# Two multiplications of constants at the head of each one-block expert

## The chip, the cores and the metric

The kernel runs on one core of a Trainium2 chip. Its time is device microseconds from the start to the end of one execution. TensorE (PE, with its weight loads PEld), VectorE (DVE), ScalarE (ACT), GpSimd (POOL) and SyncE (SP, which issues the transfers) have queues of their own and wait for each other by semaphores.

## The reference

Two transformer blocks over 256 tokens of 1024 values, all in float32. The first has two layers, the second of which ends in a mixture of experts; the second block is one further layer. The change is in the mixture:

```
def moe_swiglu(x, router_w, w1, w3, w2):
    t = x.reshape(B * S, D)
    logits = (t @ router_w).astype(jnp.float32)
    top_v, top_i = lax.top_k(logits, TOP_K)              # 2 of 8
    gates = jax.nn.softmax(top_v, axis=-1)
    combine = jnp.sum(one_hot(top_i, N_EXPERTS) * gates[..., None], axis=1)
    out = jnp.zeros_like(t)
    for e in range(N_EXPERTS):
        out = out + combine[:, e:e + 1] * swiglu(t, w1[e], w3[e], w2[e])
    return out

def swiglu(x, w1, w3, w2):
    return (jax.nn.silu(x @ w1) * (x @ w3)) @ w2
```

w1 and w3 of an expert are 1024 x 3584, w2 is 3584 x 1024.

## The kernel before

**Experts.** The eight experts are taken in order of the tokens they hold, the fullest first. For each the tokens that chose it are gathered into one or two blocks by a product with a matrix of picks (`gather`, `e_P`), go through the expert's three matrices, and are added back to the running sum `acc` (named b_XT in the trace) by another product (`finish`). `FORMS` gives the forms an expert may take. "n" is a plain block of up to 128 tokens. "a" is a folded block of up to 64 tokens, whose high and low parts lie side by side in one stationary operand. A form of two letters has two blocks. Which form of the list runs is chosen at run time from the counts.

**Pieces.** A weight matrix is multiplied as a high and a low part. SyncE loads 1 MB halves into four ring buffers; ScalarE rounds a piece of 128 x 2048 values to its high part (`e_hi`, line 2371), VectorE subtracts to get the low part (`e_lo`, line 1901), and TensorE multiplies both by the block: lines 993, 994 and 995 in a plain block (three products, 12 to a piece), lines 998 and 999 in a folded one (two products, 8 to a piece). There are places for three split pieces; ScalarE may split piece p when TensorE is done with p - 3 (`split_round`), VectorE follows (`split_rest`), TensorE waits for that (`take_piece`). ScalarE and VectorE are told to split p + 2 at the step in which TensorE takes p. An expert has 42 pieces. They come in units of 512 hidden columns (`steps_of`): w1 in two pieces into bank 0, w3 in two pieces into bank 2, then the hidden values are turned ("T", line 1017 or 629) and multiplied by two pieces of w2 into banks 4 and 5. In a folded block ScalarE copies bank 0 out, TensorE adds the two halves of the block up again (the doubling product, line 1077), and ScalarE takes SiLU of that.

**From one expert to the next.** During its last pieces an expert with one block gathers the next one's tokens into banks 0 and 2, and adds the expert before it back (`finish`, lines 1127 and 1128). After its last piece ScalarE scales the result out of banks 4 and 5 (`e_yh`), VectorE makes the rest (`e_yl`, line 1422), and, as there is no second block, VectorE's queue then raises the semaphores that a second block would have raised, `acc_add[1]` the last of them (line 2140). At its head each expert but the first waits on TensorE for `acc_add[1]` of the one before, then for its gathered rows (`gath_l[0]`), and then does its first product, into bank 0, which also waits for its piece.

**Multiplications of constants.** `keep_up(n, b)` multiplies the identity by the first 512 columns of the constants n times into bank b; nobody reads the result. The kernel has it at seven places outside the experts' loop (line 642). Each f32 multiplication leaves two records of a matmul in the trace.

The order of the instructions is written out by hand, each engine's in its own function.

Of the kernel before, what the change touches and what calls it, by code (L numbers as in the profile page):

```python
# [209 lines left out]
def block_of(ex, s):  # L210

    return (ex + s) % 2
# [57 lines left out]
def two_blocks(nc, a):  # L270
    ctx = ExitStack()
    with ctx:
# [344 lines left out]
        def pe(e):  # L617
# [21 lines left out]
            def keep_up(n, b):  # L639

                for _ in range(n):
                    e.matmul(bank[b][:, :], ident, cst[:, 0:512], start=True, stop=True)
# [461 lines left out]
            def gather(ex, s, g, b):  # L1104

                e.wait_ge(*pick[s](ex))
                for c in range(4):
                    ins = sums(bank[b][:, tok(c)], [(X[:, t, tok(4 * g + c)], e_P[s][:, t, :]) for t in range(2)])
                ins.then_inc(gath[s].sem)

            def turn_picks(ex, s, b):

                e.wait_ge(*pick[s](ex))
                turn(bank[b], [e_P[s][:, t, :] for t in range(2)])
                sums(bank[b][:, 256:257], [(e_P[s][:, t, :], comb[:, t, ex:ex + 1]) for t in range(2)]).then_inc(pt_turn[s].sem)

            def finish(ex, banks):

                e.wait_ge(*y_dve[0](ex))
                e.wait_ge(*y_act[0](ex))  # L1120
                if ex:
                    e.wait_ge(*acc_add[0](ex - 1))
                pt = e_PT[0][ex % 3]
                for t in range(2):
                    for n in range(2):
                        b = bank[banks[2 * t + n]]
                        e.matmul(b[:, :], pt[:, tok(t)], e_yh[:, half(n)], start=True, stop=False)
                        e.matmul(b[:, :], pt[:, tok(t)], e_yl[:, half(n)], start=False, stop=True).then_inc(back[0].sem)

            def finish_second(ex):  # L1130

                e.wait_ge(*y_dve[1](ex))
                e.wait_ge(*y_act[1](ex))
                for t in range(2):
                    for n in range(2):
                        e.matmul(bank[2 * t + n][:, :], e_PT[1][0][:, tok(t)], e_h[n][:, :], start=True, stop=True).then_inc(back[1].sem)

            def expert(ex, kinds, wide, hints, on):

                unit, more, tiles = 6 + 7 * ex, ex + 1 < NE, len(kinds)  # L1140
                if ex:
                    e.wait_ge(*acc_add[1](ex - 1))
                if tiles == 1:
                    e.sem_inc(gath[1].sem, 2)
                    e.sem_inc(pt_turn[1].sem, 1)
                    e.sem_inc(back[1].sem, 4)
                if tiles == 2 and ex:
                    e.wait_ge(*gath_l[0](ex))
                    e.wait_ge(*pt_out[0](ex))
                    if ex > 1:  # L1150
                        e.wait_ge(*acc_add[0](ex - 2))
                    for g in range(2):
                        gather(ex, 1, g, 2 + g)
                    turn_picks(ex, 1, 1)
                e.wait_ge(*gath_l[0](ex))

                def first(kind, s):
                    if kind == "w1":
                        return [gath_l[1](ex), pt_out[1](ex)] if s else []
                    if kind == "w3":  # L1160
                        return [gath_l[1](ex)] if s else [pt_out[0](ex)]
                    if ex and tiles == 2:
                        return [acc_add[0](ex - 1)]
                    return [y_dve[0](ex - 1), y_act[0](ex - 1)] if ex else []

                def aside(kind, u, hf):
                    if more and len(FORMS[ex + 1]) == 2 and kind == "T" and u == 3:
                        hints.append(e.mark_branch_hint_location(hint=wide[ex + 1]))
                    if tiles == 2 and kind == "T" and u == 6:
                        on.append(e.mark_branch_hint_location())  # L1170
                    if ex and tiles == 2 and (kind, u, hf) == ("w1", 0, 1):
                        finish(ex - 1, (4, 5, 6, 7))
                    if more and tiles == 1 and kind == "T" and u == 4:
                        if ex > 1:
                            e.wait_ge(*acc_add[0](ex - 2))
                        turn_picks(ex + 1, 0, 6)
                    if tiles == 1 and (kind, u, hf) == ("d", 5, 1):
                        if more:
                            gather(ex + 1, 0, 0, 0)
                            e.wait_ge(*tl_out(unit + 6))  # L1180
                            gather(ex + 1, 0, 1, 2)
                        if ex:
                            if more:
                                e.wait_ge(*pt_out[0](ex + 1))
                            finish(ex - 1, (6, 7, 1, 3))
                    if more and tiles == 2 and kind == "T" and u == 6:
                        for g in range(2):
                            gather(ex + 1, 0, g, g)
                        e.wait_ge(*tl_out(unit + 6))
                        turn_picks(ex + 1, 0, 2)  # L1190

                gated(FFE_UNITS, MOE_P + 42 * ex, unit, kinds, first, aside, [block_of(ex, s) for s in range(2)])
                if "a" not in kinds:
                    e.sem_inc(g_both.sem, 7)
                if tiles == 2:
                    if more:
                        e.wait_ge(*gath_l[0](ex + 1))
                        e.wait_ge(*pt_out[0](ex + 1))
                    finish_second(ex)

            def experts():
# [10 lines left out]
                for ex in range(NE):  # L1212
                    if len(FORMS[ex]) == 1:
                        expert(ex, FORMS[ex][0], wide, hints, [])
                        continue
                    branch = e.br_eq(wide[ex], 0, on_true=f"narrow{ex}", on_false=f"wide{ex}")
                    for place in hints:
                        branch.branch_hint(place)
                    hints = []
                    with nc.body(f"wide{ex}", valid_engines=[e.engine]):  # L1220
                        on = []
                        expert(ex, FORMS[ex][1], wide, hints, on)
                        end = e.br(f"done{ex}")
                        for place in on:
                            end.branch_hint(place)
                    with nc.body(f"narrow{ex}", valid_engines=[e.engine]):
                        on = []
                        expert(ex, FORMS[ex][0], wide, hints, on)
                        end = e.br(f"done{ex}")
                        for place in on:  # L1230
                            end.branch_hint(place)
                    nc.switch_bb(f"done{ex}")
# [1890 lines left out]
```

## Time and profile before

| | |
|---|---|
| median of 3 runs | 2141.49 us (2138.68 to 2147.89) |
| the profiled execution | 2139.3 us; span from first to last instruction 2137.5 us |
| busy in the span | PE 93%, PEld 73%, DVE 71%, ACT 52%, POOL 3% |
| mean granted clock of TensorE | 0.985 of full |
| chain that ended last, by engine | PE 72%, DVE 13%, issue 7%, ACT 7%, POOL 1% |
| records of line 642 (constants) | 94, that is 47 multiplications |
| experts 1 to 7, first product of 1 to last of 7 | 947.72 to 1783 us |

A busy PE is not PE at its peak. The chain is followed back from the last instruction, at each step to what released it. A share of the span is an average over stages with different limits, so the stretch around the change is read by itself.

### The profile page before, as it was taken

How to read it: one execution, taken by the hardware profiler on the slowest of the kernel's cores; microseconds unless marked ns; L12 is line 12 of the kernel's file. 1: busy time of each engine (PE TensorE's matmuls, PEld its weight loads, DVE VectorE, ACT ScalarE, POOL GpSimd, SP SyncE). 2: the span in 40 equal slices, each digit the busy share in tenths (PEclk: the TensorE clock that was granted, in tenths of full speed). 3: DMA queues.
4: the chain of work that ended last, by engine and by line, in shares of the span. 5: the costliest groups of instructions: out<-in, count | busy, mean ns of one | idle time of the engine just before them, and what ended most of it. 6: DMA issues, size and time to landing. Idle time of an engine off the chain costs nothing.

```text
span 2137.5 us, 25380 instructions
## 1 busy us (share of the span) xinstructions
PE 1998.2 (93%) x9950; PEld 1562.1 (73%) x9950; DVE 1511.9 (71%) x1835; ACT 1101.8 (52%) x1144; POOL 58.0 (3%) x64
## 2 busy tenths in 40 slices
PE   8989999999899999999999998988988898999997
PEld 7568588876596788878878766666666666659997
DVE  4665645447575655568888898998899898646666
ACT  1233244412230344447677777877777773545554
POOL 0120000000400000000000000000000000100000
PEclk9999999999999899999999999999999999999999
DMA  8201264433000666659989899999999994316450
GB/s 332 79 1 52 110 252 177 157 144 118 1 1 1 262 230 211 217 180 369 362 320 367 332 403 348 404 358 381 392 356 403 345 401 169 119 64 255 166 205 20
DMA packets 65018, 484.42 MB, mean 227 GB/s; under 512 B 9840, under 2 KB 12912, under 8 KB 13680
## 3 DMA queue, kind: packets, MB, share of 16 engines
q1 hardware_dynamic: 64880, 482.58, 59.6%
q8 instruction: 87, 1.43, 0.3%
q14 instruction: 51, 0.42, 0.1%
HBM read 481.51 MB, written 1.05 MB: 226 GB/s over the span
## 4 chain that ended last, share of the span: by engine, by line
PE 72%; DVE 13%; issue 7%; ACT 7%; POOL 1%; DMA 0%; DVEq 0%; SPq 0%; ACTq 0%; POOLq 0%
PE bank L622 12%; PE bank L993 11%; PE bank L995 11%; PE bank L994 11%; PE bank L998 7%; PE bank L999 6%; PE bank L825 5%; ACT e_hi L2371 4%; DVE e_lo L1901 4%; PE bank L1017 2%; PE bank L1077 2%; PE bank L786 1%; PE bank L629 1%; DVE b_arena L1416 1%; DVE e_h L1416 1%
## 5 line engine op out<-in xcount | busy, mean ns | idle before, releaser
L1901 DVE TENSOR_TENSOR e_lo<-b_ring,e_hi 128x2048 fp32r<-128x2048 f32 (+1 forms) x407 | 921.1, 2280 | 286.5 <-ACT e_hi L2371 285.5
L2371 ACT ACTIVATE e_hi<-b_ring 128x2048 fp32r<-128x2048 f32 (+1 forms) x407 | 772.1, 1909 | 200.2 <-PE bank L995 114.3
L998 PE MATMUL bank<-e_hi,e_x 128*128 128x512 f32 x672 | 277.9, 414 | 34.7 <-DVE e_lo L1901 24.8
L999 PE MATMUL bank<-e_lo,e_x 128*128 128x512 f32 x672 | 264.2, 393 | 0.0
L993 PE MATMUL bank<-e_hi,e_x 128*128 128x512 f32 (+1 forms) x528 | 209.6, 397 | 5.9 <-DVE e_lo L1901 4.4
L994 PE MATMUL bank<-e_lo,e_x 128*128 128x512 f32 (+1 forms) x528 | 203.8, 386 | 0.0
L995 PE MATMUL bank<-e_hi,e_x 128*128 128x512 f32 (+1 forms) x528 | 203.8, 386 | 0.0
L998 PEld LDWEIGHTS bank<-e_hi,e_x 128*128 128x128 f32 x672 | 126.7, 189 | 101.8 <-DVE e_lo L1901 60.9
L998 PE MATMUL bank<-e_hi,e_th 128*128 128x512 f32 x336 | 137.9, 410 | 20.7 <-DVE e_lo L1901 20.1
L999 PEld LDWEIGHTS bank<-e_lo,e_x 128*128 128x128 f32 x672 | 127.0, 189 | 25.0 <-issue 1.8
L993 PE MATMUL bank<-e_hi,e_th 128*128 128x512 f32 x352 | 137.8, 391 | 0.4 <-DVE e_tl L1905 0.4
L994 PE MATMUL bank<-e_lo,e_th 128*128 128x512 f32 x352 | 137.2, 390 | 0.0
L995 PE MATMUL bank<-e_hi,e_tl 128*128 128x512 f32 x352 | 137.1, 389 | 0.0
L999 PE MATMUL bank<-e_lo,e_th 128*128 128x512 f32 x336 | 131.6, 392 | 0.0
L622 PE MATMUL bank<-b_ring,b_XT 128*128 128x512 f32 (+1 forms) x320 | 128.3, 553 | 1.5 <-issue 1.5
L993 PEld LDWEIGHTS bank<-e_hi,e_x 128*128 128x128 f32 x528 | 100.4, 190 | 27.9 <-issue 9.2
L994 PEld LDWEIGHTS bank<-e_lo,e_x 128*128 128x128 f32 x528 | 100.4, 190 | 20.4 <-issue 1.7
L995 PEld LDWEIGHTS bank<-e_hi,e_x 128*128 128x128 f32 x528 | 100.1, 190 | 20.3
L2371 ACT ACTIVATE b_arena<-bank 128x512 f32<-128x512 f32 (+2 forms) x96 | 46.0, 511 | 132.3 <-PE bank L629 67.6
L993 PE MATMUL bank<-e_x,e_hi 128*128 128x256 f32 x384 | 108.9, 284 | 2.0 <-DVE e_x L1905 1.9
L995 PE MATMUL bank<-e_x,e_lo 128*128 128x256 f32 x384 | 108.7, 283 | 0.0
L994 PE MATMUL bank<-e_x,e_hi 128*128 128x256 f32 x384 | 108.7, 283 | 0.0
(268 smaller groups left out, 2852.8 us busy)
## 6 DMA issues: line engine op xcount, KB each, us to landing
b_ring<-in_moe_w SPq DMA_DIRECT2D x336, 1024.0 KB, 7.0
b_ring<-in_ffn_w SPq DMA_DIRECT2D x15, 2048.0 KB, 8.4
b_ring<-in_w_in SPq DMA_DIRECT2D x14, 2048.0 KB, 8.1
b_ring<-in_w_up SPq DMA_DIRECT2D x12, 2048.0 KB, 8.3
b_ring<-in_w_down SPq DMA_DIRECT2D x6, 2048.0 KB, 8.2
b_ring<-in_w_o SPq DMA_DIRECT2D x4, 2048.0 KB, 8.2
b_gain<-in_gains SPq DMA_DIRECT2D x6, 1024.0 KB, 4.5
b_ring<-in_w_out SPq DMA_DIRECT2D x2, 2048.0 KB, 8.5
```

The source lines that it names most:

```text
L622: ins = e.matmul(out, x, y, start=start and i == 0, stop=stop and i == len(pairs) - 1)
L825: last = e.matmul(heads(b)[:, h, :], *f(h), start=True, stop=True)
L993: e.matmul(out, ah, bh, start=first, stop=False)
L994: e.matmul(out, ah, bl, start=False, stop=False)
L995: return e.matmul(out, al, bh, start=False, stop=last)
L998: e.matmul(out, both, bh, start=first, stop=False)
L999: return e.matmul(out, both, bl, start=False, stop=last)
L1017: ins = e.matmul(bank[2 + s][:, 64 * c:64 * c + 64], e_h[s][:, tok(c)], pairs[:, 0:64], start=True, stop=True)
L1077: e.matmul(bank[s][:, 0:w], pairs, e_h[s][:, 0:w], start=True, stop=True).then_inc(g_both.sem)
L1416: return e.tensor_tensor(out, x, y, op)
L1901: e.tensor_tensor(lo, raw, r32(hi), ALU.subtract).then_inc(lo_dve.sem)
L2371: return e.activation(out, x, ACT.Copy)
```

## The change

Behind the two waits at the head of an expert that isn't the first and has one block, TensorE multiplies constants twice into bank 0. The first product after it starts a new sum in that bank.

```
                     turn_picks(ex, 1, 1)
                 e.wait_ge(*gath_l[0](ex))
+                if ex and tiles == 1:
+                    keep_up(2, 0)
 
                 def first(kind, s):
                     if kind == "w1":
```

TensorE's order at the head of a plain expert with one block (b_cst are the constants, e_x the gathered block; s_st_out carries `acc_add[1]`, s_dec_in `gath_l[0]`, s_lo_dve the low part; the branch closes the other form of the expert):

```order
-L1223 UNCONDITIONAL_BRANCH
-L993 MATMUL bank0<-e_hi0,e_x 128x512 [waits s_st_out,s_lo_dve,s_dec_in]
+L1225 UNCONDITIONAL_BRANCH
+L642 MATMUL bank0<-b_cst 128x512 [waits s_st_out,s_dec_in]
+L642 MATMUL bank0<-b_cst 128x512
+L993 MATMUL bank0<-e_hi0,e_x 128x512 [waits s_lo_dve]
 L994 MATMUL bank0<-e_lo0,e_x 128x512
```

The two waits have moved from the first product to the first multiplication of constants; the product keeps its wait for the piece. TensorE's order at the head of a folded expert, the eighth:

```order
-L1229 UNCONDITIONAL_BRANCH
-L998 MATMUL bank0<-e_hi0,e_x 128x512 [waits s_st_out,s_lo_dve,s_dec_in]
+L1231 UNCONDITIONAL_BRANCH
+L642 MATMUL bank0<-b_cst 128x512 [waits s_st_out,s_dec_in]
+L642 MATMUL bank0<-b_cst 128x512
+L998 MATMUL bank0<-e_hi0,e_x 128x512 [waits s_lo_dve]
 L999 MATMUL bank0<-e_lo0,e_x 128x512
```

The same two come in front here, before the pairs of lines 998 and 999. No other engine's order changes.

## Rows read from the trace of the kernel before

**Rows 1.** Stretches of experts 1, 2, 4, 5, 7: length, busy by engine, PEclk, DMA share.
```profile
947.72:1071.75 124.03, 124.03 (x578) 103.02 (x578) 105.91 (x66) 86.80 (x57) 0.00 (x0) 1.00 0.92 342
1074.23:1199.90 125.67, 125.67 (x578) 104.19 (x578) 107.17 (x69) 87.64 (x58) 0.00 (x0) 0.99 0.93 346
...
1317.85:1432.16 114.31, 102.50 (x452) 75.41 (x452) 104.39 (x67) 87.56 (x65) 0.00 (x0) 1.00 0.97 381
1434.55:1550.56 116.01, 103.62 (x452) 76.70 (x452) 104.49 (x67) 87.64 (x65) 0.00 (x0) 0.99 0.96 375
...
1669.74:1783.00 113.26, 98.86 (x414) 71.04 (x414) 104.67 (x65) 85.33 (x64) 0.00 (x0) 1.00 0.95 370
```

**Rows 2.** TensorE's timeline, heads of experts 1 to 4: start, length, instruction, [idle before, releaser].
```profile
947.72 0.47 PE L993 MATMUL bank<-e_hi,e_x 128*128 128x512 f32 x1 [1.32 <-DVE b_XT L1416]
...
1074.23 0.59 PE L993 MATMUL bank<-e_hi,e_x 128*128 128x512 f32 x1 [2.49 <-DVE e_lo L1901]
...
1202.38 0.47 PE L998 MATMUL bank<-e_hi,e_x 128*128 128x512 f32 x1 [2.48 <-DVE e_lo L1901]
...
1317.85 0.47 PE L998 MATMUL bank<-e_hi,e_x 128*128 128x512 f32 x1 [2.48 <-DVEq L2140]
```

**Rows 3.** Line 2140 by source: its records, and who waited for it.
```profile
L2140 DVEq EVENT_SEMAPHORE  x7: 21/21/21, 1073.6 to 1782.0; - x7
...
  PE bank L998: 9.7, 4
```

**Rows 4.** Chain of waits around the head of expert 4: start, length, what.
```profile
1317.14 0.02 DVEq L2140
```

**Rows 5.** VectorE's timeline before the head of expert 2.
```profile
1066.95 2.29 DVE L1901 TENSOR_TENSOR e_lo<-b_ring,e_hi 128x2048 fp32r<-128x2048 f32 x1 [1.12 <-ACT e_hi L2371]
...
1069.16 2.47 DVE L1416 TENSOR_TENSOR b_XT<-b_XT,bank 128x512 f32<-128x512 f32 x4
...
1071.55 2.29 DVE L1901 TENSOR_TENSOR e_lo<-b_ring,e_hi 128x2048 fp32r<-128x2048 f32 x1
```

**Rows 6.** TensorE's timeline, third piece of experts 4 and 5.
```profile
1321.14 0.39 PE L998 MATMUL bank<-e_hi,e_x 128*128 128x512 f32 x1
1321.37 0.39 PE L999 MATMUL bank<-e_lo,e_x 128*128 128x512 f32 x1
1322.82 0.50 PE L998 MATMUL bank<-e_hi,e_x 128*128 128x512 f32 x1 [1.06 <-DVE e_lo L1901]
...
1439.62 0.50 PE L998 MATMUL bank<-e_hi,e_x 128*128 128x512 f32 x1 [1.16 <-DVE e_lo L1901]
```

**Rows 7.** Stretches behind the heads of experts 2 and 3.
```profile
1074.50:1077.80 3.30, 3.30 (x9) 2.55 (x9) 2.87 (x3) 0.55 (x1) 0.00 (x0) 0.50 0.92 293
...
1202.38:1207.95 5.57, 5.57 (x24) 4.58 (x25) 4.57 (x4) 4.20 (x4) 0.00 (x0) 1.00 0.81 247
```

**Rows 8.** TensorE's timeline: constants at full and half clock, doubling product of expert 3.
```profile
1914.00 3.60 PE L642 MATMUL bank<-b_cst 128*128 128x512 f32 x8
...
712.69 3.61 PE L642 MATMUL bank<-b_cst 128*128 128x512 f32 x4
...
1207.95 1.02 PE L1077 MATMUL bank<-e_h,b_cst 128*128 128x512 f32 x2
1208.87 0.50 PE L998 MATMUL bank<-e_hi,e_x 128*128 128x512 f32 x1
```

**Rows 9.** ScalarE's timeline behind the head of expert 4.
```profile
1320.03 1.92 ACT L2371 ACTIVATE e_hi<-b_ring 128x2048 fp32r<-128x2048 f32 x1 [1.50 <-PE bank L999]
...
1322.33 1.91 ACT L2371 ACTIVATE e_hi<-b_ring 128x2048 fp32r<-128x2048 f32 x1
1325.91 0.60 ACT L2374 ACTIVATE e_h<-bank 128x512 f32<-128x512 f32 x1 [1.66 <-PE bank L1077]
```

**Rows 10.** VectorE's timeline behind the head of expert 4.
```profile
1320.48 6.69 DVE L1901 TENSOR_TENSOR e_lo<-b_ring,e_hi 128x2048 fp32r<-128x2048 f32 x3
1328.35 2.29 DVE L1901 TENSOR_TENSOR e_lo<-b_ring,e_hi 128x2048 fp32r<-128x2048 f32 x1 [1.18 <-ACT e_hi L2371]
```

More of the change, by code:

```diff
@@ L1155, in expert @@
                 e.wait_ge(*gath_l[0](ex))
+                if ex and tiles == 1:
+                    keep_up(2, 0)
                 def first(kind, s):
```

## The prediction

> **What bounds the kernel now.** The page comes first: it has TensorE as the engine of most of the chain that ended last, so time added to TensorE counts unless something else is late at that place. The table by stretch tells the seven experts concerned apart [rows 1]; each stretch runs from the first product of an expert to its last. In experts 1 and 2, the two plain ones, PE is busy for 124.03 of 124.03 us and 125.67 of 125.67 us: every microsecond put in front shifts all that follows. In experts 3 to 7, the folded ones (4, 5 and 7 are shown), PE is busy for 98.86 to 103.62 of 113 to 116 us, and VectorE for 104.39 to 104.67: there the round from ScalarE (high part) to VectorE (low part) to TensorE (product) and back, through three places for split pieces, sets the pace.
>
> Next the heads. PE's timeline has the first product of each expert with the idle time before it [rows 2]: 1.32 us at expert 1 and about 2.5 us at the other six (three of them are shown). What ends it decides this case. Line 2140, the event by which VectorE's queue tells that the second block (which isn't there) was added back, is named four times as what TensorE waited for, with 9.7 us [rows 3]; at expert 4 it stands at 1317.14 [rows 4], 0.7 us before the first product. At experts 2 and 3 the row names a low part (e_lo) instead. That is a coincidence of times: the first product needs piece 0 of the expert, and in VectorE's order piece 0 is split before the four additions to b_XT; the part split after them, which ended last, is piece 1 [rows 5]. The first event of line 2140, at 1073.6, lies as far before the product at 1074.23 as it does at expert 4.
>
> Last, what comes behind the head. In experts 4 to 7 TensorE does two pieces and stands again before the third, for 1.06 to 1.16 us (four times; the first two are shown), until VectorE has its low part [rows 6]. At expert 3 there is no such gap: PE is busy for 5.57 of 5.57 us up to the doubling product, line 1077 [rows 7].
>
> **The change part by part.** It removes nothing, moves nothing on SP, ACT, DVE or POOL, and adds two multiplications of the identity by 512 columns of constants, in f32, at the head of experts 1 to 7. All seven ran with one block in the profile (line 2140, which only such experts have, comes seven times [rows 3]), so 14 are added. In the order of instructions they take over the two waits, on the addition (s_st_out) and on the gathered rows, that the first product had, and the product keeps only the wait for its piece. So they start when the product started before, not in the idle time. Behind them on TensorE's queue is every product of the expert, and VectorE and ScalarE wait for these.
>
> Price of a pair. The same instruction comes before in rows of four: 8 records (two to a multiplication) in 3.60 us at the full clock [rows 8], of which the last 0.16 us overlaps whatever follows: 0.86 us each. One f32 product of that shape between others, line 1077, puts the next one off by 1208.87 - 1207.95 = 0.92 us (same rows). A pair is thus 1.72 to 1.84 us; I take 1.8.
>
> Experts 1 and 2: nothing hides it, TensorE being busy without a gap from there to the end of the expert. 1.8 each. At the head of expert 2 the clock stands at 0.50 of full from just behind the first product [rows 7], and this expert is 125.67 - 124.03 = 1.64 us longer than expert 1. With the pair there, it is the pair that runs slowly: at half clock a pair takes 3.61 us [rows 8], and the products give back their 1.64, net 1.97. That is so near to 1.8 that I keep 1.8.
>
> The Trainium skill ("TensorE: Matmul & The Clock Gate", Part 1) says that the slow state is the default and that activity releases it. By this rule feeding TensorE something before the real products is worth while, if it comes while TensorE would stand. The trace agrees on the state (0.50 behind the idle time of expert 2, 1.00 behind that of expert 3 [rows 7]), but here the pair stands behind the idle time, which is over when it starts; by the rule the sum stays as it is, less a clock loss at best.
>
> Expert 3: pieces 0, 1 and 2 come without a gap, so the doubling product is 1.8 us late, ScalarE's SiLU behind it and its next high part too, and VectorE had waited for that one. 1.8.
>
> Experts 4 to 7: the pair fills the gap before the third piece. The gap is 1.06 to 1.16 us by its row and 0.16 more, since a product of 0.39 us has the next one start 0.23 us behind its own start where nothing is waited for (1321.14 and 1321.37 in the same rows): 1.22 to 1.32. What is left of 1.8 is 0.58 at expert 4 and 0.48 to 0.5 at the others, 2.0 us for the four. Is that all that goes on? ScalarE's high part of piece 3 starts at 1320.03, when piece 0 has freed its place [rows 9]; it moves to 1321.8, the high part of piece 4 from 1322.33 to 1324.1, VectorE's low part of piece 3 from about 1322.7 to 1323.7: one microsecond. But the low part of piece 5, from which the rest of the expert hangs, waited for ScalarE, at 1328.35 with VectorE idle before it [rows 10], and ScalarE's SiLU at 1325.91 for the doubling product, which follows the third piece; those move by the 0.6 alone, and VectorE's three low parts still end in time for it (1323.7 and three times 2.2 is 1330.3 where piece 5 ends now at 1330.56). So 0.5 to 0.6 each, with 1.0 as the upper end where VectorE's backlog counts (2 us more in all, within my forecast). Nothing behind it gives time back: VectorE is busy for some 104 of 114 us, and its waits hang from ScalarE, which hangs from TensorE.
>
> Bounds. Below: in experts 4 to 7 it is hidden altogether, 3 x 1.72 = 5.2 us. Above: the full 1.84 at all seven, 12.9 us. Below nothing it goes only if half-clock stretches vanish; that is a rival. The DMA queue has more time, not less; its share of 0.92 to 0.97 in these stretches [rows 1] falls.
>
> Sum: 1.8 + 1.8 + 1.8 + 2.0 = 7.4 us on a profiled execution of 2139.3 us (span 2137.5 and 1.8 around it): 2146.7. The median of the three runs shown, 2141.49, lies 2.2 us above that execution, so 2148.9 against the median. I forecast 2149 us, 0.35% more.
>
> **The rivals.** A: the heads of the folded experts fall to half clock. Then the pair takes 3.61 us there [rows 8], of which the gap hides 1.3, and 2.3 are left instead of 0.5. For it: one head of seven did fall, and expert 5 holds another such stretch a little behind its head, 116.01 us against 114.31 at expert 4 [rows 1]; every head has the same 2.4 us of idle time. Before, such a stretch at a folded head cost little, since the third piece waited anyway. Against it: experts 1, 4 and 7 stayed at 1.00 throughout, and the pair closes one gap behind the head. Price: two such heads give 5.4 + 2 x 2.3 + 2 x 0.5 = 11.0, all four 14.6: 2152 to 2156 us. It decides from two heads on, where 10.7 us (0.5%) are passed.
>
> B: hidden in all folded experts, because the pace there is VectorE's. For it: PE has some 11 us of slack in each. Against it: TensorE's slack is scattered behind waits on VectorE, and the third piece's gap is too short. Price: 5.4 us, 2147.
>
> C: not slower. The pair keeps TensorE at full clock: were the waits over earlier than I read (if the head waited for e_lo, as two rows name, the pair, which doesn't, would run in the idle 2.4 us and cost nothing), the half-clock stretches behind the heads would go, 1.64 each; expert 2 and expert 5 show one each, so 3.3 us are gained: 2138. It decides if the pair starts over 1.8 us before the first product's old place. Against it: the event of line 2140, and that both waits of the product move to the pair. A rule of the skill's same page (Part 2, "Step-by-step") is that matmuls keep their program order and only weight loads are pulled ahead. By it a product can't pass the pair either; in the row of line 1077 the next product starts 0.92 us behind, in order.
>
> **How the numbers follow.** My forecast gets 0.57, A 0.25, B 0.11 and C 0.07. About 0.5% (10.7 us) is what a measurement of this kernel can tell from no change: the runs before lie 9.2 us apart. The forecast and B fall within 0.5%, save for some 0.03 that noise lifts above; A lies above; of C half a part in seven may end as faster by over 0.5%. That gives slower 0.28, same 0.70, faster 0.02. For the range, 0.1 is left out on either side: from 2143, which holds B and the quieter half of the noise, to 2156, which holds A at all four heads. The likeliest case alone has 2145 to 2153.
>
> **What would show it.** In the profile after: 122 records of line 642 where 94 are now, 28 of them in the heads; the first of each pair at the place of the old first product behind 2.4 us of idle; the first product 1.7 to 1.9 us later (3.6 where the clock is at half); experts 1 and 2 with PE still busy throughout; no gap before the third piece in experts 4 to 7, or one under 0.3 us; the low part of piece 5 late by 0.5 to 1.0. The forecast is wrong if the pair lies inside the idle time, or if experts 4 to 7 grow by over 1.2 us each at full clock, or don't grow.

## The result, and the profile after

The changed kernel takes 2149.06 us in the median of 22 runs (2138.64 to 2157.3), the kernel before 2141.57 (2130.27 to 2147.89). The ratio is 1.0036, with a 95% interval of 1.0024 to 1.0048: slower by 7.5 us between the medians and 7.7 by the ratio, and clear of no change. The profiled execution has a span of 2147.4 us.

The page after, its first lines:

```profile
span 2147.4 us, 25429 instructions
...
PE 2017.2 (94%) x9978; PEld 1569.8 (73%) x9978; DVE 1512.6 (70%) x1835; ACT 1102.1 (51%) x1144; POOL 58.1 (3%) x64
```

PE has 28 records more than before and is busy for 19 us more; DVE and ACT are busy for the same time. TensorE's timeline at the heads of experts 1 to 6, answering to [rows 2]; columns as there:

```profile
943.74 1.95 PE L642 MATMUL bank<-b_cst 128*128 128x512 f32 x4 [1.17 <-DVE b_XT L1418]
...
1071.80 1.96 PE L642 MATMUL bank<-b_cst 128*128 128x512 f32 x4 [2.34 <-DVEq L2142]
1073.19 0.79 PE L993 MATMUL bank<-e_hi,e_x 128*128 128x512 f32 x1
...
1199.91 3.36 PE L642 MATMUL bank<-b_cst 128*128 128x512 f32 x4 [2.33 <-DVEq L2142]
...
1318.63 2.62 PE L642 MATMUL bank<-b_cst 128*128 128x512 f32 x4 [2.34 <-DVEq L2142]
1320.26 1.42 PE L998 MATMUL bank<-e_hi,e_x 128*128 128x512 f32 x1
1321.47 0.63 PE L999 MATMUL bank<-e_lo,e_x 128*128 128x512 f32 x1
...
1437.36 1.95 PE L642 MATMUL bank<-b_cst 128*128 128x512 f32 x4 [2.35 <-DVEq L2142]
1438.75 0.79 PE L998 MATMUL bank<-e_hi,e_x 128*128 128x512 f32 x1
1439.38 0.39 PE L999 MATMUL bank<-e_lo,e_x 128*128 128x512 f32 x1
...
1554.33 2.79 PE L642 MATMUL bank<-b_cst 128*128 128x512 f32 x4 [2.24 <-DVEq L2142]
```

The idle time is still there, and the pair stands behind it. Line 2142 is what line 2140 was [rows 3]: VectorE's event. The source view of it now names the pair, at six heads of seven (expert 1 has no such event ahead of it; its row names b_XT):

```profile
L2142 DVEq EVENT_SEMAPHORE  x7: 21/21/21, 1071.3 to 1785.4; - x7
...
  PE bank L642: 13.8, 6
```

Stretches after: from the pair of expert 5 to its doubling product, then the ones behind the pairs' start at experts 4, 2 and 1 (columns as in [rows 1]; 1.00 and 0.50 are the two levels of TensorE's granted clock):

```profile
1437.36:1444.62 7.26, 7.26 (x28) 5.34 (x29) 6.46 (x5) 4.18 (x4) 0.00 (x0) 1.00 0.76 248
1319.90:1323.10 3.20, 3.20 (x7) 1.99 (x6) 3.20 (x4) 0.00 (x0) 0.00 (x0) 0.50 0.62 166
1071.80:1075.20 3.40, 3.40 (x11) 2.15 (x12) 3.29 (x3) 0.96 (x1) 0.00 (x0) 1.00 0.78 241
943.74:947.00 3.26, 3.26 (x11) 2.04 (x12) 2.29 (x1) 0.00 (x0) 0.00 (x0) 1.00 0.01 3
```

The gap before the third piece [rows 6] is gone: PE is busy for 7.26 of 7.26 us. And this time it is the heads of experts 3, 4 and 6 that fall to half clock, not that of expert 2: their pairs take 3.36, 2.62 and 2.79 us, those at full clock 1.95 or 1.96. Rounds of expert 5 behind its head, answering to [rows 9, 10], ScalarE's timeline:

```profile
1441.25 1.92 ACT L2373 ACTIVATE e_hi<-b_ring 128x2048 fp32r<-128x2048 f32 x1 [3.08 <-PE bank L999]
1443.08 0.58 ACT L2373 ACTIVATE e_h<-bank 128x512 f32<-128x512 f32 x1
1443.55 1.91 ACT L2373 ACTIVATE e_hi<-b_ring 128x2048 fp32r<-128x2048 f32 x1
1445.74 0.60 ACT L2376 ACTIVATE e_h<-bank 128x512 f32<-128x512 f32 x1 [0.28 <-PE bank L1077]
```

and VectorE's:

```profile
1440.12 2.28 DVE L1903 TENSOR_TENSOR e_lo<-b_ring,e_hi 128x2048 fp32r<-128x2048 f32 x1
1443.20 4.58 DVE L1903 TENSOR_TENSOR e_lo<-b_ring,e_hi 128x2048 fp32r<-128x2048 f32 x2 [0.80 <-ACT e_hi L2373]
1448.19 2.29 DVE L1903 TENSOR_TENSOR e_lo<-b_ring,e_hi 128x2048 fp32r<-128x2048 f32 x1 [0.40 <-ACT e_hi L2373]
```

VectorE's three low parts in one row of 6.69 us are now one, an idle 0.80 us, and two; the low part of piece 5 begins 1448.19 - 1437.36 = 10.83 us behind the head's first instruction. Before, it began 1328.35 - 1317.85 = 10.50 behind it at expert 4, and 1445.13 - 1434.55 = 10.58 at expert 5 itself; VectorE's row of that one, from the trace before:

```profile
1445.13 2.29 DVE L1901 TENSOR_TENSOR e_lo<-b_ring,e_hi 128x2048 fp32r<-128x2048 f32 x1 [1.16 <-ACT e_hi L2371]
```

**Lengths of the experts.** Single microseconds are not read from whole times here (the runs of one kernel lie up to 20 us apart) but from the length of one expert. It is the time from the end of one expert's last product to the end of the next one's; that end is the start of the row at the head less the idle time in its brackets (1317.85 - 2.48 = 1315.37 and 1434.55 - 2.39 = 1432.16 give 116.79 for expert 4 before). Where a pair of the experiments lies in the idle time itself, the product before the pair is taken. "h" marks a half-clock stretch that begins within 4 us of the head, "t" one that begins some 15 us behind it, at the first turn.

| expert | 1 | 2 | 3 | 4 | 5 | 6 | 7 |
|---|---|---|---|---|---|---|---|
| before | 125.35 | 128.15 h | 115.47 | 116.79 | 118.40 t | 116.79 | 112.90 |
| after | 126.89 | 128.13 | 118.71 h | 118.72 h | 117.07 | 118.59 h | 113.02 |
| pair at 1 to 3 | 127.12 | 128.13 | 118.75 h | 116.98 h | 116.97 h | 116.81 | 112.82 |
| pair at 4 to 7 | 125.30 | 128.14 h | 115.44 | 116.99 | 116.89 | 118.57 h | 112.95 |
| one, not two | 126.05 | 128.91 h | 117.92 h | 116.79 | 116.80 | 118.38 t | 112.87 |
| four, not two | 128.59 | 131.63 h | 118.75 | 118.58 | 120.35 h | 118.61 | 116.37 h |
| pair in the idle time | 125.59 | 126.57 | 115.47 | 118.35 t | 116.89 | 118.36 t | 112.79 |
| three in the idle time | 125.31 | 126.57 | 119.39 h | 118.45 t | 118.41 t | 116.79 | 114.43 t |
| pair at the turn | 125.34 | 128.16 h | 115.87 | 116.77 | 117.13 h | 117.19 h | 112.85 |
| idle time and turn | 125.35 | 126.57 | 115.87 | 116.80 | 116.76 | 116.72 | 112.86 |

The sum over the seven is 833.9 us before and 841.1 after: 7.3 us. The other 2.6 us between the two spans lie outside these seven experts, where no instruction changed. Each row of the table is one profiled execution.

### The profile page after: what moved, and what is told of

It is laid out like the page before. It is cut to its first block, busy times and chain, and to the rows that moved or that the text cites. A ratio compares the mean times of both kernels' runs of the same rounds, so it can differ in the third digit from the quotient of the medians.

```text
span 2147.4 us, 25429 instructions
## 1 busy us (share of the span) xinstructions
PE 2017.2 (94%) x9978; PEld 1569.8 (73%) x9978; DVE 1512.6 (70%) x1835; ACT 1102.1 (51%) x1144; POOL 58.1 (3%) x64
## 4 chain that ended last, share of the span: by engine, by line
PE 73%; DVE 12%; issue 7%; ACT 7%; POOL 1%; DMA 0%; DVEq 0%; SPq 0%; ACTq 0%; POOLq 0%
PE bank L622 12%; PE bank L993 11%; PE bank L995 11%; PE bank L994 11%; PE bank L998 7%; PE bank L999 6%; PE bank L825 5%; ACT e_hi L2373 4%; DVE e_lo L1903 4%; PE bank L1017 2%; PE bank L1077 2%; PE bank L629 1%; PE bank L786 1%; DVE b_arena L1418 1%; DVE e_h L1418 1%
```

## The experiments

My theory: the pair costs what TensorE's path takes of it, all where there is no gap behind the head, little where there is one. Against it stood an equal price at every head, an entire hiding in the folded experts, and a cost that is mostly half clock.

**The pair at experts 1 to 3 alone.**

```
-                if ex and tiles == 1:
+                if 0 < ex < 4 and tiles == 1:
                     keep_up(2, 0)
```

> The pair stays at the heads of experts 1 to 3 and goes from those of experts 4 to 7. If the pair costs what TensorE's path takes of it (1.6 us where TensorE has no gap behind the head): 3 x 1.6 = 4.9 us over before, 0.23%, so ratio 1.0023. Rival, every head costs a seventh of the 7.5 us measured: 3.2 us, 1.0015. Rival, the cost is mostly half clock at the folded heads: 2 us or less, 1.0009.

Measured 1.0018 (0.9997 to 1.0038), which separates none of the three. The lengths do: expert 2 takes 128.13 without a half-clock stretch, 1.56 more than the 126.57 of the kernels that have no pair behind the wait at its head and no half clock there (the pair is in the idle time, below). Expert 1 pays 1.77 here (127.12), where it paid 1.54 in the changed kernel; the idle time at its head is 1.42 us here and 1.17 there, and in one kernel without a pair at that head it is 1.59 instead of 1.32. Experts 4 and 5 of this kernel show something else. Their heads, without a pair, fell to half clock; TensorE's timeline, and the stretch behind it:

```profile
1321.78 0.47 PE L998 MATMUL bank<-e_hi,e_x 128*128 128x512 f32 x1 [2.39 <-DVEq L2142]
```

```profile
1323.00:1326.20 3.20, 3.20 (x9) 2.42 (x9) 3.20 (x4) 1.50 (x1) 0.00 (x0) 0.50 0.61 156
```

They take 116.98 and 116.97 us, 0.2 more than the 116.79 to 116.80 at full clock: the gap before the third piece swallows the slow products.

**The pair at experts 4 to 7 alone.**

```
-                if ex and tiles == 1:
+                if ex > 3 and tiles == 1:
                     keep_up(2, 0)
```

> The pair stays at the heads of experts 4 to 7 and goes from those of experts 1 to 3. By the path, the gap before the third piece takes 1.2 to 1.3 us of each pair: 0.3 to 0.6 each, 1.2 to 2.4 us, and up to 1.2 more for each of these heads that falls to half clock: 1.0006 to 1.0022. Rival, every head costs the same: 4.3 us, 1.0020 without any half clock at these heads. Rival, hidden: 1.0000.

Measured 1.0021 (1.0001 to 1.0041). The ratio lies at the upper end of what I expected and on the rival's 1.0020, so whole times don't tell these two apart; a pair hidden altogether is outside the interval. By the two ratios, wide as their intervals are, the four folded heads cost no less in all than the first three. By lengths, experts 4, 5 and 7 are 0.05 to 0.2 us longer, less than I expected. But expert 6, whose head fell to half clock, takes 118.57 instead of 116.79. The head, and the stretch behind it:

```profile
1546.17 2.67 PE L642 MATMUL bank<-b_cst 128*128 128x512 f32 x4 [2.24 <-DVEq L2142]
```

```profile
1547.40:1550.60 3.20, 3.20 (x7) 1.91 (x6) 3.20 (x4) 0.00 (x0) 0.00 (x0) 0.50 0.62 164
```

The same stretch at half clock costs a folded expert 0.2 us without the pair and 1.6 to 1.8 with it (here, and at experts 4 and 6 after). The pair has used the gap up. That this is what whole times show as well is likely but not counted: how many folded heads fell in the runs without a profile is not on record.

**Four and one instead of two.** In one kernel `keep_up(4, 0)`, in another `keep_up(1, 0)` in the same place.

> Four multiplications of constants instead of two at each of the seven heads. By the path: 3.3 us at each of experts 1 to 3, and 3.3 - 1.25 = 2.1 at each of experts 4 to 7, since the gap there is used up by the first pair: 9.9 + 8.4 = 18.3 us, ratio 1.0085, more than twice the 7.5 us of one pair. Rival, each multiplication costs the same: 15 us, 1.0070.

> One multiplication of constants instead of two at each of the seven heads. By the path: 0.75 us (half of 1.6) at each of experts 1 to 3, 2.3 us, and nothing at full clock at experts 4 to 7, where the gap of 1.2 to 1.3 us before the third piece holds all of it: lengths of experts 4 to 7 within 0.1 us of before where no half-clock stretch lies in them, ratio 1.0008 to 1.0015. Rival, each multiplication costs the same everywhere: half of what the pair costs, 3.7 us, 1.0018, and experts 4 to 7 longer by 0.1 to 0.15 each.

Measured: four 1.0092 (1.0064 to 1.0120), one 1.0012 (0.9994 to 1.0030). Neither ratio tells the two expectations apart. The lengths at full clock do: with one, expert 1 gains 0.70 and experts 4, 5 and 7 nothing (116.79, 116.80, 112.87). With four, experts 1 and 3 gain 3.24 and 3.28, experts 4 and 6 gain 1.79 and 1.82. So at the heads with a gap the first multiplication is free, the second costs 0.05 to 0.3, and the third and fourth cost 1.5 to 1.8 together; at the others each costs 0.7 to 0.9. An equal price at every head is out. With one multiplication the gap is smaller but still there; TensorE's timeline at expert 5 of that kernel:

```profile
1434.21 1.10 PE L642 MATMUL bank<-b_cst 128*128 128x512 f32 x2 [2.24 <-DVEq L2142]
...
1439.42 0.50 PE L998 MATMUL bank<-e_hi,e_x 128*128 128x512 f32 x1 [0.44 <-DVE e_lo L1903]
```

**The pair inside the idle time.** At the end of a one-block expert, ahead of the wait for the addition:

```
                 gated(FFE_UNITS, MOE_P + 42 * ex, unit, kinds, first, aside, ...)
 ...
+                if tiles == 1 and more:
+                    e.wait_ge(*gath_l[0](ex + 1))
+                    keep_up(2, 0)
```

> The pair goes from the head (behind the wait for the addition) to the end of the one-block expert before it, in front of that wait and behind the one for the gathered rows alone: six pairs, ahead of experts 2 to 7. By the path it lies in the 2.4 us in which TensorE stands anyway: no added time, first products where they were, 0.7 us of idle left, and perhaps one or two half-clock stretches at the heads fewer (1.6 us each): ratio 0.9985 to 1.0003. Rival, the multiplications cost by being there (their code, their weights, the bank): 6/7 of 7.5 us, 1.0030.

Measured 0.9992 (0.9973 to 1.0011), which leaves out the rival's 1.0030. TensorE's timeline at expert 2:

```profile
1065.75 1.88 PE L642 MATMUL bank<-b_cst 128*128 128x512 f32 x4
1068.40 0.47 PE L993 MATMUL bank<-e_hi,e_x 128*128 128x512 f32 x1 [0.77 <-DVE e_lo L1904]
```

Six pairs here, and no cost where the clock stays up: expert 2 takes 126.57 us, expert 3 115.47 as before. No head of this kernel's experts 2 to 7 fell to half clock; two first turns did (t). In the next, `keep_up(3, 0)` stands in the same place:

> Three multiplications instead of two in the idle time ahead of the wait. Three take 2.6 us, and 0.67 us of idle time are left behind two. By the path the first product of experts 2 to 7 comes 0.1 to 0.3 us later, which experts 2 and 3 pay and the gap before the third piece hides in 4 to 7: ratio 0.999 to 1.0005. Rival, the idle time itself is needed by something (the branch's code, the semaphores' way): over 0.8 us at experts 2 and 3.

Measured 1.0016 (0.9994 to 1.0039), and inconclusive as a whole time. Experts 2 and 4 to 7 show no cost beside their t. Expert 3 shows a stop that I had not expected, which the view calls "issue", so no wait that the profile shows (the rival had named over 0.8 us at experts 2 and 3; it came at 3 and not at 2):

```profile
1195.80 2.74 PE L642 MATMUL bank<-b_cst 128*128 128x512 f32 x6
1200.72 0.47 PE L998 MATMUL bank<-e_hi,e_x 128*128 128x512 f32 x1 [2.19 <-issue]
```

It came at one of six heads; its cause is open.

**The first turn.** What remained was the t (three such stretches in two profiles by then): 1.82 us of idle time ahead of the first turn of a folded expert. TensorE's row at expert 5 in the trace before:

```profile
1448.08 1.11 PE L1017 MATMUL bank<-b_cst,e_h 128*128 128x64 f32 x8 [1.82 <-DVE e_h L1416]
```

A pair there, alone and with the one in the idle time at the head:

```
                     if kind == "T":
+                        if kinds == "a" and u == 0:
+                            keep_up(2, 7)
                         for s in range(tiles):
```

> The kernel before with only the pair ahead of the first turn of each folded expert. If the idle time ahead of the turn lowers the clock: no half-clock stretch 15 us behind a head, those at the heads as before (1.6 us at experts 1 to 3, 0.2 at 4 to 7): ratio 0.9985 to 1.0000. Rival as for the pair in both places: 1.0000 to 1.0007.

> The pair in the idle time ahead of the wait, and a second pair into bank 7 in the 1.82 us of idle time ahead of the first turn of each folded expert, where a stretch at half clock began in three of the profiles (15 us behind the first product). If that idle time is what lowers the clock there, no half-clock stretch is left in experts 2 to 7, 1.6 us less for each that was there, one to two in a run: ratio 0.9980 to 0.9995, and lengths of 115.7, 116.8, 116.8, 116.8 and 112.9 us in experts 3 to 7. Rival, the second pair puts the turn off (it starts when its wait is over, and the pair can still be under way): 0.1 to 0.3 us at each of five experts and no gain, 1.0000 to 1.0007.

Measured: the turn alone 1.0016 (0.9999 to 1.0032), with both 0.9975 (0.9956 to 0.9993). The turn alone lies above what I expected, and is not clear of no change. No t is left in its profile, but heads fall (h) and now cost experts 5 and 6 0.3 and 0.4; expert 3, where only 1.2 us were idle ahead of the turn, pays 0.4 for the pair. That is the rival's price, at one of its five experts. With both, the clock stays up in all seven. Stretches of that kernel, within experts 2 to 7:

```profile
1066.73:1192.30 125.57, 125.57 (x582) 103.76 (x582) 108.64 (x69) 88.94 (x61) 0.00 (x0) 1.00 0.95 351
1195.00:1308.00 113.00, 104.05 (x454) 75.48 (x452) 102.50 (x66) 88.21 (x67) 0.00 (x0) 1.00 0.98 381
1310.50:1424.00 113.50, 103.68 (x454) 75.60 (x453) 103.56 (x68) 87.41 (x65) 0.00 (x0) 1.00 0.97 381
1425.90:1541.00 115.10, 105.09 (x459) 76.75 (x460) 105.20 (x68) 88.38 (x67) 0.00 (x0) 1.00 0.97 380
1542.00:1657.00 115.00, 104.35 (x457) 76.56 (x458) 104.91 (x66) 88.30 (x65) 0.00 (x0) 1.00 0.97 381
1658.00:1769.00 111.00, 100.49 (x418) 71.48 (x417) 102.49 (x63) 84.15 (x62) 0.00 (x0) 1.00 0.96 370
```

**Two more idle times.** To the kernel with both, a pair ahead of the adding back of expert 0's second block and three multiplications ahead of that of expert 7.

> The kernel with the pair ahead of the wait and ahead of the first turn, and the constants also in the two idle times left around the experts: a pair ahead of the adding back of expert 0's second block (2.02 us of idle time, a half-clock stretch right behind it in all ten profiles so far), and three ahead of the adding back of expert 7 (3.45 us, likewise). If idle time that lies in front of TensorE's work lowers the clock and a pair inside it prevents that, no half-clock stretch is left from expert 0's end to expert 7's, and 1.6 us less at each of the two places: ratio 0.9955 to 0.9980. Rival: the constants delay what they stand before, no change against the kernel without these two: 0.9970 to 0.9985, the stretches at about 934 and 1774 us still there.

Measured 0.9991 (0.9972 to 1.0010), above what I expected and above the rival. The two stretches at half clock are gone, but expert 1's head comes later (1.85 us of "issue" ahead of its first product instead of 1.32), and expert 1 takes 125.88 instead of 125.35. TensorE's timeline there:

```profile
936.20 1.88 PE L642 MATMUL bank<-b_cst 128*128 128x512 f32 x4
938.39 3.67 PE L1138 MATMUL bank<-e_h,e_PTb 128*128 128x512 f32 x8 [0.31 <-ACT e_h L2381]
943.91 0.47 PE L993 MATMUL bank<-e_hi,e_x 128*128 128x512 f32 x1 [1.85 <-issue]
```

Both were run once more on one chip:

> The kernel with the pair ahead of the wait and ahead of the first turn once more, beside the one with two more idle times filled. By the lengths of the experts in the profiles (830.9 us for experts 1 to 7 with no half-clock stretch, 830.6 for the kernel before less its stretches, of which one to three come in a run at 1.6 us): ratio 0.9980 to 0.9992. Rival, the 0.9975 measured first was the whole of the gain or more: 0.9965 to 0.9978. Rival, it was the scatter of the runs: 1.0000.

> The kernel with all four idle times filled once more. By the path: like the one with two, less what the two half-clock stretches at expert 0's end and expert 7's end cost there, 1.6 us each at the most: ratio 0.9970 to 0.9990, not above the one with two. Rival, the constants delay what they stand before there (0.5 us at expert 1's head and 1 us ahead of the last adding back): equal to the one with two or above it by up to 0.0007.

Measured 0.9988 (0.9970 to 1.0005) and 0.9993 (0.9975 to 1.0010). The kernel with pairs in the idle time and at the turn was under the kernel before both times, once clear of no change and once not; against the changed kernel with its 1.0036 it is better beyond doubt. The two places more give nothing that these runs can tell, and the lengths of the first kernel come back to within 0.1 us (830.8 and 830.9 us over the seven). That its clock stays up is not a matter of the profiled execution: over whole runs TensorE's granted clock is 0.988 in the mean in both series of 12, against 0.984 in the 103 runs of the kernel before that were taken beside the experiments, and 0.983 with the pair at the turn alone.

## Why the prediction was right

**The wait and the place.** Right. The pair starts where the product started, behind VectorE's event. That the idle time is the place where it would have been free was shown by moving it there.

**The price of a pair.** Forecast 1.8 us, measured 1.54 at expert 1 (126.89 - 125.35; 1.77 in one other kernel) and 1.56 at expert 2 (128.13 - 126.57). The pair puts the products off by 1.72: the second product comes at 1439.38 - 1437.36 = 2.02 us behind the head's first instruction, where it came 0.30 behind. But the pair mostly starts 0.15 us sooner than a product did (idle time of 2.34 for 2.48 and 2.49, 1.17 for 1.32); at some heads it is less (2.35 for 2.39 at expert 5). That small gain I had not in the sum.

**Expert 3.** Right: no gap, the full price; 118.71 is 115.47 and two terms of 1.6, the pair and the stretch at half clock. At full clock, four multiplications cost it 3.28, twice 1.64.

**Experts 4 to 7.** The step was right, its size was not: 0.5 us forecast for each at full clock, 0.05 to 0.3 measured (117.07 and 113.02 after; 116.99, 116.89 and 112.95 with the pair at these four alone). The backlog of about one microsecond on VectorE's low part of piece 3 came, and ended ahead of piece 5, as worked out. But that low part, forecast to be late by 0.5 to 1.0, is late by 0.25 at expert 5 (10.83 for 10.58), and expert 5 is longer by 0.27 to 0.28. Most of the difference is the price: 1.57 less the 1.22 to 1.32 that the gap was worked out to take is 0.25 to 0.35. Why some heads pay less still is open.

**The clock.** My sum took it as the same in both; rival A said that a folded head at half clock would cost 2.3 us instead of 0.5 and that two such heads were needed. Its mechanism is what the runs show, at 1.8 to 1.9 us for such a head, pair and stretch together; the profile after has two of these heads (4 and 6), so by its own condition A is what that execution shows. So the 7.4 us of the forecast and the 7.3 of the profile have different terms: three times 1.6 at experts 1 to 3 (4.7), four times about 0.2 (0.7), three stretches at half clock of 1.6 now (4.9) less two of 1.64 before (3.3): 7.0. That the sums agree so well is luck in part; two terms were too large and one was missing. And these terms are those of two executions. Over whole runs half clock is no more frequent after the change: the granted clock is 0.984 in the mean of the 22 runs, as in the 103 runs before. So a third stretch is not what the change brings on the whole; what it can bring is that a stretch at a folded head costs 1.6 instead of 0.2. How much of the 7.5 us between the medians that makes is not shown. How often a folded head falls is not settled: in the profiles of the seven kernels that leave its idle time open it did so at between none and two heads of four.

**The rivals.** B, hidden in all folded experts, holds nearly at full clock (0.05 to 0.3 us each) and fails at half clock. C, a pair that runs in the idle time, is what the kernel would have to be rewritten for; then it does hold the clock up there.

## What to carry to other kernels

Work that is to keep an engine awake has to stand in front of the wait that makes it idle; behind the wait it is work on the path like any other. Where a gap downstream seems to hide it, ask what else that gap hid before: here it had covered the stretches at half clock. And a price of one or two microseconds in two thousand is read from the length of one stage between two fixed points, marked by its clock, not from whole times.

## What the runs showed of the hardware

- The granted clock fell to 0.50 behind idle times of 1.8 to 3.5 us, but not behind each. In the profiles of the seven kernels that leave the 2.2 to 2.6 us ahead of the heads of experts 2 to 7 idle, it fell at 17 of 42 heads. In the six that have multiplications of constants there, it fell at one of 36, the one behind which TensorE stood for another 2.19 us; 0.7 us of idle time left did no harm.
- Behind VectorE's event a multiplication of constants, with two waits, mostly started after 0.44 us, and a product, with three, after 0.59; at some heads either came 0.1 us later. Whether the number of waits makes the difference was not tested.
- Ahead of a first product behind a branch, "issue" without a wait rose to 2.19 us once (three multiplications in the idle time, expert 3) and to 1.85 us in one kernel, both times that it ran (expert 1). The cause is open.
